# Which weight units pass through a side buffer: the next expert's two down units in place of its first gate/up quarter

## The reference, cut to what matters

```
h = RMSNorm(x) * (1 + scale2) + shift2
top-4 of 32 experts per token, softmax over the chosen router logits
for each expert e, on its tokens:
    gu   = h @ w_gu[e] + b_gu[e]                    # (1024 x 2048)
    gate = min(gu[:, :1024], 7); up = clip(gu[:, 1024:], -7, 7)
    act  = (up + 1) * gate * sigmoid(1.702 * gate)
    out += weight * (act @ w_down[e] + b_down[e])   # (1024 x 1024)
x = x + gate2 * out
```

## Time and profile before

| | us |
|---|---|
| median of 3 runs | 1631.74 |
| the profiled execution's own time | 1629.55 |
| its span in the profile | 1627.9 |
| MoE loop, q1 of expert 1 to q1 of expert 31 | 588.3 to 1547.8 |
| PE busy in the span | 1403.2 |
| PE idle until a piece of q0 is copied (L2208) | 134.1 in 12 waits |
| POOL busy in the span | 183.9 |

### The profile page before, as it was taken

One profiled execution on the slowest core, in us unless ns is written; L12 is line 12 of the kernel. 1 busy time (PEld: TensorE's weight loads), 2 busy tenths in 40 slices (PEclk: granted clock), 3 DMA queues, 4 the chain that ended last, 5 costly groups with the idle time before them and its releaser, 6 DMA issues.

```text
span 1627.9 us, 40564 instructions
## 1 busy us (share of the span) xinstructions
PE 1403.2 (86%) x16361; PEld 758.5 (47%) x16362; DVE 624.3 (38%) x1321; ACT 247.6 (15%) x580; POOL 183.9 (11%) x240
## 2 busy tenths in 40 slices
PE   6998989999999699979999797797779797779794
PEld 3445656367676445535554353343335343334352
DVE  2334646344623534334344242332314332233334
ACT  2124532211110311101111010000001010000011
POOL 2021310000000001000110110110110110001100
PEclk9999989988999699989999898898989898899897
DMA  9734992940191379699999999999999969997940
GB/s 356 247 137 151 356 396 72 369 150 1 46 351 69 155 307 408 266 402 423 406 395 403 428 414 417 417 406 415 414 424 407 413 283 393 423 407 295 384 183 33
DMA packets 71426, 505.66 MB, mean 311 GB/s; under 512 B 6528, under 2 KB 6648, under 8 KB 35316
## 3 DMA queue, kind: packets, MB, share of 16 engines
q1 hardware_dynamic: 63588, 480.98, 73.1%
q0 software_dynamic: 7792, 24.08, 4.5%
HBM read 499.92 MB, written 5.11 MB: 310 GB/s over the span
## 4 chain that ended last, share of the span: by engine, by line
PE 72%; DMA 17%; DVE 6%; issue 1%; ACT 1%; POOL 1%; SPq 1%; DVEq 0%; ACTq 0%; POOLq 0%
PE psum L533 67%; DMA region<-in_w_gu 13%; DMA ring<-in_w_down 2%; PE psum L697 2%; DMA ring<-in_w_ada 2%; PE psum L1018 1%; PE psum L993 1%; DVE region L1315 1%; POOL ring L2208 1%; DMA ring<-in_w_gu 1%; DVE region L1164 1%; PE psum L729 0%; ACT region L1819 0%; DVE region L1282 0%; SPq L2273 0%
## 5 line engine op out<-in xcount | busy, mean ns | idle before, releaser
L533 PE MATMUL psum<-ring,region 128*32 128x256 f32 (+2 forms) x11264 | 744.6, 390 | 138.1 <-POOL ring L2208 134.1
L533 PEld LDWEIGHTS psum<-ring,region 128*32 128x32 f32 (+1 forms) x11264 | 370.5, 112 | 460.2 <-POOL ring L2208 165.6
L1819 ACT ACTIVATE region<-psum 128x256 f32<-128x256 f32 (+5 forms) x330 | 136.7, 417 | 1149.5 <-PE psum L533 503.6
L533 PE MATMUL psum<-region 128*32 128x256 f32 (+11 forms) x2700 | 253.2, 424 | 19.1 <-DVE region L1208 9.0
L2208 POOL COPY ring<-region 128x1024 f32<-128x1024 f32 x124 | 123.8, 1041 | 919.7 <-DMA region<-in_w_gu 744.4
L1729 DVE TENSOR_TENSOR region<-region,psum 128x1280 f32<-128x1280 f32 x110 | 163.2, 1484 | 165.8 <-PE psum L533 165.8
L533 PE MATMUL psum<-region,ring 128*128 128x320 f32 (+1 forms) x640 | 170.3, 421 | 1.4 <-DVE region L1570 1.4
L1699 DVE TENSOR_SCALAR region<-psum,region 128x320 f32<-128x320 f32 x55 | 30.3, 551 | 355.7 <-PE psum L533 355.7
L533 PEld LDWEIGHTS psum<-region 128*32 128x32 f32 (+5 forms) x2700 | 101.5, 138 | 129.3 <-issue 91.8
L533 PEld LDWEIGHTS psum<-region,ring 128*128 128x128 f32 x640 | 117.2, 193 | 48.8 <-issue 5.5
L1685 DVE TENSOR_SCALAR region<-region 128x32 f32<-128x32 f32 x168 | 34.7, 266 | 106.0 <-issue 106.0
(11 more groups left out here) (301 smaller groups left out, 769.5 us busy)
## 6 DMA issues: line engine op xcount, KB each, us to landing
ring<-in_w_gu SPq DMA_DIRECT2D x97, 2048.0 KB, 11.3
ring<-in_w_down SPq DMA_DIRECT2D x64, 2048.0 KB, 11.3
region<-in_w_gu SPq DMA_DIRECT2D x31, 2048.0 KB, 17.3
ring<-in_w_ada SPq DMA_DIRECT2D x12, 2048.0 KB, 13.8
ring<-in_w_in SPq DMA_DIRECT2D x11, 2048.0 KB, 19.3
ring<-in_cache_k SPq DMA_DIRECT2D x64, 256.0 KB, 5.0
ring<-in_cache_v POOLq DMA_DIRECT2D x64, 256.0 KB, 5.2
ring<-in_w_out SPq DMA_DIRECT2D x2, 2048.0 KB, 21.3
```

What stands on the lines that cost most here:

```text
L533: return pe.matmul(out, lhsT, rhs, start=start, stop=stop, skip_group_check=True)
L1819: return act.activation(out, src, ACT.Copy)
```

## The change

Two landing places instead of one, for d0 and d1 of the next expert; q0 is requested straight into its ring slot as q1 to q3 are. SP's list for expert e becomes q0(e), q1(e), q2(e), q3(e), then d0(e+1) to the first place once POOL has moved d0(e) out of it, then d1(e+1) to the second likewise. POOL's wait for a slot is now `unit_read[4 + i]`, that is the down of the last block of e-1, which PE does in the first block of e. PE's down waits for all four pieces of each unit, and gate_up_quarter for the DMA's semaphore in all four quarters.

The second place lies in `region` over router scratch and split_rows, which are in use until the weights of the slots have been split (L1717 to L1720) and the "bd" banks drained. So there is a new semaphore weight_rows_ready, and before the loop SP waits for `tables`, the eight "bd" banks and weight_rows_ready, then requests d1(1). Some small tiles move within `region`.

```diff
-LANDINGS = 1
+LANDINGS = 2
...
+        landing = [region[:, REGION + KT * NT - UNIT:REGION + KT * NT], Area(E.at).take(UNIT)]
...
             def gate_up_quarter(c, expert):
 
-                if c >= LANDINGS:
-                    pe.wait_ge(unit_landed[moe_slot[c]], 16 * expert + (landed_base[c] + 16))
+                pe.wait_ge(unit_landed[moe_slot[c]], 16 * expert + (landed_base[c] + 16))
...
-                        if c < LANDINGS:
-                            pe.wait_ge(piece_moved[c], PIECES * expert + (2 * j + q + 1))
...
             def down(expert):
                 for half in range(2):
                     i = 4 + half
-                    pe.wait_ge(unit_landed[moe_slot[i]], 16 * expert + (landed_base[i] + 16))
+                    pe.wait_ge(piece_moved[half], PIECES * expert + PIECES)
...
+            dve.tensor_copy(plan_row[0:1, 0:1], plan_row[0:1, 1:2]).then_inc(weight_rows_ready, 1)
...
             for i in range(LANDINGS):
-                pool.wait_ge(unit_landed[moe_slot[i]], landed_base[i] + 16)
+                pool.wait_ge(unit_landed[moe_slot[4 + i]], landed_base[4 + i] + 16)
...
                 for i in range(LANDINGS):
-                    pool.wait_ge(unit_landed[moe_slot[i]], landed_base[i] + 16)
-                    pool.wait_ge(unit_read[i], before)
+                    pool.wait_ge(unit_landed[moe_slot[4 + i]], landed_base[4 + i] + 16)
+                    pool.wait_ge(unit_read[4 + i], before)
                     pool.wait_ge(landing_filled[i], filled)
                     for piece in range(PIECES):
                         part = slice(UNIT // PIECES * piece, UNIT // PIECES * (piece + 1))
-                        pool.tensor_copy(ring[:, moe_slot[i], part], landing[i][:, part])\
+                        pool.tensor_copy(ring[:, moe_slot[4 + i], part], landing[i][:, part])\
                             .then_inc(piece_moved[i], 1)
...
-                sp.dma_start(landing[i], gu[expert, i].rearrange("o p f -> p (o f)")).then_inc(landing_filled[i], 16)
+                sp.dma_start(landing[i].rearrange("p (c f) -> p c f", c=2),
+                             dn[expert, i].rearrange("o p c f -> p (o c) f")).then_inc(landing_filled[i], 16)
...
-                    elif i < LANDINGS:
+                    elif i >= RING - LANDINGS:
                         continue
...
             sp.wait_ge(tables, 1)
+            for m in range(KT):
+                sp.wait_ge(*drained("bd", m))
+            sp.wait_ge(weight_rows_ready, 1)
+            fill_landing(1, slice(1, 2))
```

More of the change, by code:

```diff
@@ L265, in build @@
         selwT = E.take(NT)
+        pos = E.take(3, ROUNDS * NE)
         E.at = max(E.at, fin_at + KT * NT + 2 * FF)
         late_const = E.take(n_const - n_late)
+        wts = E.take(3, NE)
+        fin_ss = E.take(6)
+        fin_rstd = E.take(3)
+        plan_row = E.take(N_LIST)
+        fin_gain = E.take(D)
+        landing = [region[:, REGION + KT * NT - UNIT:REGION + KT * NT], Area(E.at).take(UNIT)]
         logits = E.take(3, NE)
         mask = E.take(3, NE)
-        wts = E.take(3, NE)
         eq = E.take(3, NE)
@@ L286, in build @@
         begun = E.take(N_LIST)
[L287 to L290, removed]
         x1_sq = Area(REGION - KT * NT).take(KT, NT)
-        landing = [region[:, REGION + KT * NT - UNIT:REGION + KT * NT]]
         assert E.at <= REGION - KT * NT
-        pos = E.take(3, ROUNDS * NE)
+        assert E.at <= REGION + KT * NT - UNIT
         y_out = h2_tok
@@ L380, in build @@
         bias_in = sem("bias_in")
+        weight_rows_ready = sem("weight_rows_ready")
         landing_filled = [sem(f"landing_filled{i}") for i in range(LANDINGS)]
```

## The result

The changed kernel takes 1682.17 us (median of 4 runs, 1673.07 to 1686.15) against 1631.96 in the same comparison; ratio 1.0299, 95% interval 1.0267 to 1.0332. The forecast was 1671.4 within 1645 to 1695. The profiled execution took 1678.89 us, its span 1676.9, 49.0 us over the span before.

The account below looks back on a forecast made before the run. The prediction took the weight stream's DMA to bound one-block experts and PE three-block ones, with two-block near 31.2 us. Loop +36.6 and start +3.1 gave +39.7 us, from 1631.7 to 1671.4, range 1645 to 1695.

Parts of the forecast that it names:

- What bounds the kernel: Before the change: DMA limits one-block experts, PE three-block ones, two-block near 31.2 us; 15 two-block, 12 one-block among 27.
- Part 1, the loop: From q1(e) landed to q1(e+1): reading, d0's copy, refills, q0 and q1 form a 31.7 us chain; +36.6 us over 27 experts.
- The cold term: PE starts slow after idling in starved experts: 12 of the 27 pay 0.7 us more, 0.3 on the mean.
- Part 2: The 248 copies: POOL has room, and slowing of DVE is taken as 0, at most 0.4 us per expert.
- the port price: GpSimd copies delaying DVE's two-operand instructions at the block's end: taken as 0, at most 0.4 us per expert.
- Parts 3 and 4: Requesting q0 direct saves 0, its waits being DMA's; three-block experts stay at PE's 46.7 us, 0, queue stops shrinking.
- Part 5, the start: Before expert 1, q0(1) lands behind d1(1), so q1(1) lands at 591.4 against 588.3: +3.1 us.
- Part 6, the end: After q1(31), the last transfers become q2 and q3, but three blocks of PE follow either way: 0.
- What would show it: Signs in the profile after: 31 to 32 us rounds, DMA stops of 1 to 3 us per expert, shorter long stops.

Follow-up runs that it names:

- experiment 1: Changed kernel with each 2 MB landing-place refill sent as four 0.5 MB requests, each as soon as its own piece was copied out: 1655.66 us.
- experiment 6: Changed kernel with both landing places' refills requested by GpSimd in its own DMA queue behind each copy, not in SP's list: 1650.18 us.
- experiment 8: Changed kernel with three extra GpSimd copies of 512 columns ahead of d0's pieces, none ahead of d1's: 1725.20 us.
- the second trace: The changed kernel run and profiled once more, nothing altered: median 1676.70 us, span of the trace 1675.5.
- experiment 3: Against the changed kernel's two landing places, one for d0 alone, refilled behind a direct request of d1: 1653.91 us.
- experiment 4: Changed kernel with GpSimd moving only 256 of each piece's 1024 columns and leaving out the rest: 1649.42 us.

## Why the prediction was right, and where its sizes were off

- **What bounds the kernel**: right, with 15 two-block and 12 one-block experts as counted; every trace has these rounds.
- **Part 1, the loop** (+36.6 forecast, +40.2 measured over the 27 short rounds). Step by step, warm: request 8.2 us behind q1's landing forecast, 8.1 measured; d1 landed 13.4 us behind d0's request, measured 8.0 + 5.6 = 13.6; then 2 x 4.9 in both. 31.4 us against 31.5. The 9.4 us to landing that I took from the rows for d1's late request measured 9.0 to 10.6, mean 9.65, at 3.5 to 4.5 us of lead. d0's request, at 1.7 us of lead, took 7.5 to 8.4. Experiments 1 and 6 (request made free of the copy: -26 and -32 us) and 8 (+43) carry the mechanism.
- **The cold term** was mis-sized: 0.7 us in each of 12 rounds. Measured it is 1.9 us (request at 9.9 to 10.1 us instead of 8.1) but in five of them; that the totals, 8.4 and 9.5 us, lie close is luck. Before the change a late copy fed PE four pieces, and the clock had nearly risen by the time q1 was read (6.11 us for the three units, not 7.41); now, in these five, it was still half for all of q0 and part of q1.
- **Part 2**: GpSimd is busy 305.8 us as forecast (308), and the port price came out as 0: L1752 and L1705 show no spread in the changed kernel. But that tests nothing, for no copy overlaps them there: L1752 starts 1.3 us behind the last piece, not near its end as I had it. Experiment 6 agrees with the lock of which the Trainium skill speaks ("SBUF — State Buffer", section Who interferes with whom): a cast that starts inside a copy of GpSimd ends with the copy. I had named only the two-input instruction from it; the one-input cast was hit, 27 times, and L1752 was at worst 0.92 us instead of 0.42.
- **Parts 3 and 4** (0 forecast, +0.9 measured): no gain of the direct q0 shows; PE's waits for it are still put down to DMA. The three long stops of the queue are 10.6 to 11.3 us against 10.9 to 11.8 before, so hardly "shorter" as the last part of the prediction had it, with eight units held. The +0.9 us is nearly all in the third three-block expert, whose first block was starved and cold.
- **Part 5, the start**: +3.1 forecast, +4.1 measured; the fill of d1(1) took 9.0 us to land, not 7.5.
- **Part 6, the end**: 0 forecast, +1.4 measured, +0.4 in the second trace; its cause stays open.
- **What would show it**: rounds of 31 to 32 us (31.0 to 32.4), one-block and two-block alike, hold in 22 of 27. "DMA stops of 1 to 3 us once per expert" does not: the queue stands still only behind the cold blocks (1.6 to 1.8 us) and in the rounds behind the three-block experts (0.9 to 1.3 us). In the others it never stops and still loses 1.1 to 1.8 us per refill, as a dip in the rate (262 GB/s, DMA share 0.82, from 1126 to 1130 us).

Left open: the parts of the 15 to 22 us that experiments 1, 3, 4 and 6 still have over the kernel before, and the cold clock as a cause by itself; no kernel kept PE warm through a starved block. No version ran faster than the kernel before.

## What to carry to other kernels

A prefetch place is not refilled when it has been filled, but when it has been emptied. If emptying it needs the consumer and then a copy, and other requests stand behind the refill in one ordered list, the copy is on the critical path however idle the engine that makes it. Before adding a place, write down for each request in the list what it waits for and how long before the queue runs empty it can be made; adding depth behind the request that is already the latest buys nothing (1634 to 1644 us for six to eight units here).

## What the runs showed of the hardware

- A 2 MB request of SP that is made well before its forerunner lands costs nothing: with 4.6 us of lead or more it has landed 4.8 to 5.4 us behind it in all but 9 of 1270 cases of ten traces (up to 6.3). With 2.2 to 3.4 us of lead it is 4.9 to 7.9, with 1.1 to 1.7 us 5.8 to 6.8, with 0 to 0.4 us 7.1 to 7.7, once 8.6. The cost begins well before the queue is empty, and the busy digits of the page, 9 in every slice without a long stop, do not show it; the rate does (374 to 412 GB/s).
- Two DMA queues on one core: GpSimd's requests of the same size ran beside SP's (experiment 6). One made at 902.7 us landed 19.2 us later, with SP's q0 and q1 landing in between.
- A small cast on DVE that starts inside a GpSimd copy ends with the copy (0.68 us and up to 2.16 instead of 0.17, experiment 6), while L1729, an add of 1.49 us with one operand in PSUM, ran as fast beside copies as alone.
